# Hybrid decoder layer with a 32-expert feed-forward: Silu and one VectorE product per expert, and slot lists kept by place, the most-used expert at place 1, with 128 slots at every place

## The reference, cut to what matters

```python
logits = xf @ router_w + router_b                 # 512 tokens, 32 experts
top_val, top_idx = lax.top_k(logits, 4)
gates = softmax(top_val)
# for each expert e, over the tokens that chose it:
gu = xb @ mlp1_w[e] + mlp1_b[e]                   # 1024 -> 2048, gate and up interleaved
gate, up = minimum(gu[..., ::2], 7.0), clip(gu[..., 1::2], -7.0, 7.0)
act = (up + 1.0) * gate * sigmoid(1.702 * gate)
y = act @ mlp2_w[e] + mlp2_b[e]                   # 1024 -> 1024
out[token] += gates[token, e] * y
# then x + out, and a last rmsnorm
```

## Time and profile before

| | |
|---|---|
| timed runs, median of 3 | 1603.47 us (1601.67 to 1604.37) |
| span of the profiled execution, first to last instruction | 1602.2 us |
| PE busy | 1547.4 us, 97% |
| DVE busy | 1320.1 us, 82% |
| ACT busy | 1068.4 us, 67% |
| POOL busy | 347.6 us, 22% |
| DMA | 465.30 MB, mean 290 GB/s |
| weight pieces, issue to landing | 384, 1024 KB each, median 8.0 us |

### The profile page before, as it was taken

One profiled execution on the slowest core, in us unless ns is written; L12 is line 12 of the kernel. 1 busy time (PEld: TensorE's weight loads), 2 busy tenths in 40 slices (PEclk: granted clock), 3 DMA queues, 4 the chain that ended last, 5 costly groups with the idle time before them and its releaser, 6 DMA issues.

```text
span 1602.2 us, 27288 instructions
## 1 busy us (share of the span) xinstructions
PE 1547.4 (97%) x10197; PEld 1254.4 (78%) x10198; DVE 1320.1 (82%) x1101; ACT 1068.4 (67%) x1014; POOL 347.6 (22%) x278
## 2 busy tenths in 40 slices
PE   6899999987899999999999999999999999999997
PEld 5677777765778888888888888888888888888885
DVE  5556565656498999999999999999999999999996
ACT  4635353434367777777777777777777777777774
POOL 7100000001145322212222212222222222221210
PEclk9999999998999999999999999999999999999999
DMA  6211111006399999999999999999999999999993
GB/s 198 57 54 41 54 41 54 15 2 224 153 390 367 375 391 383 385 381 361 385 379 377 386 383 377 375 372 378 371 383 376 381 380 372 372 374 373 384 375 134
DMA packets 99101, 465.30 MB, mean 290 GB/s; under 512 B 11408, under 2 KB 38192, under 8 KB 49760
## 3 DMA queue, kind: packets, MB, share of 16 engines
q1 hardware_dynamic: 86176, 429.59, 68.7%
q0 software_dynamic: 12864, 34.85, 8.3%
HBM read 448.51 MB, written 22.69 MB: 294 GB/s over the span
## 4 chain that ended last, share of the span: by engine, by line
PE 73%; DVE 2%; DMA 1%; ACT 0%; issue 0%; DVEq 0%; POOLq 0%
PE psum L1932 29%; PE psum L1960 14%; PE psum L1935 14%; PE psum L1965 7%; PE psum L1330 3%; PE psum L1922 2%; PE psum L1914 2%; DVE w_pieces_lo L1754 1%; PE psum L1948 1%; DMA xg<-h_rows,gath_i 0%; DMA w_pieces<-in_mlp_w 0%; PE psum L1346 0%; PE psum L1338 0%; DVE x L1876 0%; DMA w_pieces<-in_w_out 0%
## 5 line engine op out<-in xcount | busy, mean ns | idle before, releaser
L1754 DVE TENSOR_TENSOR w_pieces_lo<-w_pieces,w_pieces_hi 128x2048 fp32r<-128x2048 f32 x384 | 867.6, 2288 | 79.8 <-ACT w_pieces_hi L1618 79.7
L1618 ACT ACTIVATE w_pieces_hi<-w_pieces 128x2048 fp32r<-128x2048 f32 x384 | 736.1, 1919 | 220.5 <-PE psum L1935 154.1
L1932 PE MATMUL psum<-w_pieces_hi,xh 128*128 128x512 f32 x1024 | 284.3, 399 | 0.0
L1932 PE MATMUL psum<-w_pieces_hi,xl 128*128 128x512 f32 x1024 | 274.4, 390 | 0.0
L1935 PE MATMUL psum<-w_pieces_lo,xh 128*128 128x512 f32 x1024 | 274.2, 389 | 0.0
L1558 POOL DMA_INDIRECT sum_rows<-ys,this_i x30 | 143.6, 4786 | 418.2 <-ACT ys L1638 417.9
L1932 PEld LDWEIGHTS psum<-w_pieces_hi,xl 128*128 128x128 f32 x1024 | 192.2, 188 | 41.3
L1935 PEld LDWEIGHTS psum<-w_pieces_lo,xh 128*128 128x128 f32 x1024 | 192.2, 188 | 40.3
L1932 PEld LDWEIGHTS psum<-w_pieces_hi,xh 128*128 128x128 f32 x1024 | 185.3, 188 | 45.1 <-issue 11.3
L1960 PE MATMUL psum<-w_pieces_hi,ah 128*128 128x512 f32 x512 | 158.0, 390 | 0.1
L1960 PE MATMUL psum<-w_pieces_hi,al 128*128 128x512 f32 x512 | 157.7, 389 | 0.0
(11 more groups left out here) (366 smaller groups left out, 1901.9 us busy)
## 6 DMA issues: line engine op xcount, KB each, us to landing
w_pieces<-in_mlp_w SPq DMA_DIRECT2D x384, 1024.0 KB, 8.0
w_raw<-in_w_in SPq DMA_DIRECT2D x26, 512.0 KB, 4.1
w_pieces<-in_w_out SPq DMA_DIRECT2D x8, 512.0 KB, 9.2
sum_rows<-x POOLq DMA_DIRECT2D x5, 512.0 KB, 3.7
chunk_work<-in_x SPq DMA_DIRECT2D x4, 512.0 KB, 6.1
sc<-pall POOLq DMA_DIRECT2D x16, 128.0 KB, 4.0
x<-in_x SPq DMA_DIRECT2D x4, 512.0 KB, 13.6
h_rows<-w_pieces POOLq DMA_DIRECT2D x4, 512.0 KB, 2.9
```

The costliest lines, as they stand in the source:

```text
L1618: nc.scalar.activation(hi[:, p % RING], raw[:, raw_slot(b, p)].rearrange("p r n -> p (r n)"), ACT.Copy).then_inc(s_hi, 1)
L1754: nc.vector.tensor_tensor(lo[:, p % RING], raw[:, raw_slot(b, p)].rearrange("p r n -> p (r n)"), hi[:, p % RING].bitcast(F32), ALU.subtrac ...
L1932: nc.tensor.matmul(bank(up_bank(b) + c), a[:, k, :], hi[:, p % RING, c * 512:(c + 1) * 512], start=False, stop=False)
```

## The change

- The activation: ACT takes `Silu` of 1.702*gate, which is 1.702*gate*sigmoid(1.702*gate), as soon as up is clipped. DVE takes min(silu, its value at 7) times the clipped up. The product with the clipped gate (L1778) is gone, and the factor 1.702 is taken out of the gates in routing.
- Places: the experts get places. Places 0, 30 and 31 keep their experts; of experts 1 to 29 the one with most tokens changes place with expert 1. `place_of_expert` and its twin `expert_at` hold the exchange (it is its own inverse). The list keys use the place, the weight loads of SP read the expert number of a place from `expert_at` into a register, and the one-hot column that picks an expert's bias comes from `pick_at` instead of a constant table.
- Widths: places 0 and 1 have `P` = 128 slots, all others `NARROW` = 128 slots. The code that is narrower for places from 2 on is there, with a width of 128. `lists` is loaded by two DMAs (places 0 and 1; 2 to 31). PE's turns b = 2 and 3 are written out, its loop runs from 4.

The core of the diff:

```diff
+WIDE = 2
+NARROW = 128
+SILU_MAX = float(ALPHA * 7.0 / (1.0 + np.exp(-ALPHA * 7.0)))
@@ output_and_route, route_vector
-        nc.vector.tensor_tensor(rank[:, :, 0:EXPERTS], hidden[:], ranks, ALU.add)
-        nc.vector.tensor_tensor(rank[:, :, INDEXED - 1:INDEXED], hidden[:, :, EXPERTS - 2:EXPERTS - 1], ranks[:, :, EXPERTS - 2:EXPERTS - 1], ALU.add)
-        chain(nc.vector.memset(r1[:, 29:30], 0.0))
+        nc.vector.tensor_tensor(rank_at[:, :, 0:1], hidden[:, :, 0:1], ranks[:, :, 0:1], ALU.add)
+        chain(nc.vector.tensor_tensor(rank[:], hidden[:], ranks, ALU.add))
         g["select"](0, 0)
...
-        chain(nc.vector.tensor_reduce(r1[:, 20:21], bank(5, NT * EXPERTS, (NT + 1) * EXPERTS), AX.X, ALU.max))
+        chain(nc.vector.scalar_tensor_tensor(largest[:], counts, float(EXPERTS), con("among"), ALU.mult, ALU.add))
+        chain(nc.vector.tensor_reduce(r1[:, 21:22], largest[:], AX.X, ALU.max))
+        chain(nc.vector.tensor_scalar(only[:], largest[:], r1[:, 21:22], None, ALU.is_equal))
+        chain(nc.vector.tensor_tensor_reduce(moved[:], only[:], con("experts"), 1.0, 0.0, ALU.mult, ALU.add, r1[:, 22:23]))
+        chain(nc.vector.tensor_tensor(moved[:], only[:], con("to_one"), ALU.mult))
+        chain(nc.vector.tensor_tensor(place_of_expert[:], moved[:], con("experts"), ALU.add))
+        chain(nc.vector.tensor_copy(place_of_expert[:, 1:2], r1[:, 22:23]))
+        nc.vector.tensor_scalar(gates[:], gates[:], 1.0 / ALPHA, None, ALU.mult)
+        for place in range(1, 3):
+            last = nc.vector.scalar_tensor_tensor(at_place[:, place - 1], over_tokens(place_of_expert[:]), float(place), rank[:], ALU.is_equal, ALU.mult)
+        chain(last)
+        nc.vector.tensor_copy(expert_at[:], place_of_expert[:]).then_inc(g["s_order"], 1)
+        nc.vector.tensor_scalar(pick_at[:, 0:EXPERTS], place_of_expert[:], con("lane"), None, ALU.is_equal).then_inc(g["s_order"], 1)
+        nc.vector.tensor_reduce(rank_at[:, :, 1:3].rearrange("p t n -> p n t"), at_place[:], AX.X, ALU.add)
+        nc.vector.tensor_copy(rank_at[:, :, LAST_COL:RANK_COLS], rank[:, :, EXPERTS - 2:EXPERTS])
+        chain(nc.vector.scalar_tensor_tensor(largest[:], only[:], float(NARROW - P), counts, ALU.mult, ALU.add))
+        chain(nc.vector.tensor_tensor(largest[:], largest[:], con("wide_first"), ALU.subtract))
+        chain(nc.vector.tensor_reduce(r1[:, 20:21], largest[:], AX.X, ALU.max))
@@ experts, sync
+            def expert(b):
+                return sp.value_load(expert_at[0:1, bass.ds(b, 1)], min_val=0, max_val=EXPERTS - 1)
...
+            sp.wait_ge(g["s_order"], 1)
+            e = expert(1)
...
             with sp.Fori(2, EXPERTS) as b:
-                for p in range(PIECES):
-                    load(r, b, p)
+                e = expert(b - 2)
+                for p in range(DOWN):
+                    load(r, b, p, e)
+                e = expert(b)
+                for p in range(DOWN, PIECES):
+                    load(r, b, p, e)
@@ experts, gpsimd
-            nc.gpsimd.dma_start(lists[:, 0:EXPERTS, :], g["list_dram"].rearrange("(r s e) w -> r s e w", s=P, e=EXPERTS)[bass.ds(r, 1)].rearrange(
-                "a s e w -> (a s) e w")).then_inc(s_lists, 16)
-            pool.wait_ge(s_lists, r * 16 + 16)
+            rows = g["list_dram"].rearrange("(s e) w -> s e w", e=EXPERTS)
+            nc.gpsimd.dma_start(lists[:, 0:WIDE, :], rows[bass.ds(r * P, P), 0:WIDE, :]).then_inc(s_lists, 16)
+            nc.gpsimd.dma_start(lists[0:NARROW, WIDE:EXPERTS, :], rows[bass.ds(r * NARROW, NARROW), WIDE:EXPERTS, :]).then_inc(s_lists, 16)
+            pool.wait_ge(s_lists, r * 32 + 32)
@@ experts, scalar and vector
-            nc.scalar.activation(sg[:], pairs(e)[:, :, 0], ACT.Sigmoid, scale=1.702).then_inc(s_sig, 1)
+            nc.scalar.activation(sg[:], pairs(e)[:, :, 0], ACT.Silu, scale=ALPHA).then_inc(s_sig, 1)
-            nc.vector.tensor_scalar(uu[:], pairs(e)[:, :, 1], 8.0, -6.0, ALU.min, ALU.max).then_inc(s_u, 1)
-            dve.wait_ge(s_u, r * EXPERTS + (e + 1))
-            nc.vector.scalar_tensor_tensor(uu[:], pairs(e)[:, :, 0], 7.0, uu[:], ALU.min, ALU.mult).then_inc(s_x, 1)
+            nc.vector.tensor_scalar(uu[:], pairs(e)[:, :, 1], 8.0, -6.0, ALU.min, ALU.max).then_inc(s_x, 1)
-            nc.vector.scalar_tensor_tensor(av[:], sg[:], SIG_MAX, uu[:], ALU.min, ALU.mult).then_inc(s_act, 1)
+            nc.vector.scalar_tensor_tensor(av[:], sg[:], SILU_MAX, uu[:], ALU.min, ALU.mult).then_inc(s_act, 1)
@@ experts, tensor
+        def width(b):
+            return P if isinstance(b, int) and b < WIDE else NARROW
-            with pe.Fori(2, EXPERTS) as b:
+            for b in range(2, 2 + WIDE):
+                down(r, b)
+                up(r, b, True)
+            with pe.Fori(2 + WIDE, EXPERTS) as b:
```

More of the change, by code:

```diff
@@ L1114, in output_and_route @@
     stacked = carve(P, NT, 4 * EXPERTS).rearrange("p t (c e) -> p t c e", c=4).bitcast(F32R)
+    largest = carve(P, EXPERTS)
+    only = carve(P, EXPERTS)
+    moved = carve(P, EXPERTS)
+    place_of_expert = carve(P, EXPERTS)
+    at_place = carve(P, 2, NT, EXPERTS)
     w_v = d["w_out"][0].rearrange("(k p) n -> p k n", p=P)
@@ L1414, in experts @@
 def experts(nc, d, sb, sem, st, g, route, con, ident, psum, bank, out):
-    rank, info, flags, raw, bias, s_raw = (g[k] for k in ("rank", "info", "flags", "raw", "bias", "s_raw"))
+    rank_at, expert_at, pick_at, info, flags, raw, bias, s_raw = (g[k] for k in ("rank_at", "expert_at", "pick_at", "info", "flags", "raw", "bias", "s_raw"))
     x, stat, o_t, sum_dram, down_b, turned = (g[k] for k in ("x", "stat", "o_t", "sum_dram", "down_b", "turned"))
@@ L1640, in pick_bias @@
         def pick_bias(r, m):
-            nc.scalar.activation(pick[:], con("pick")[:, bass.ds(m, 1)].to_broadcast([P, P]), ACT.Copy).then_inc(s_pick, 1)
+            if not isinstance(m, int) or m:
+                act.wait_ge(g["s_order"], 2)
+            column = con("pick") if isinstance(m, int) and not m else pick_at[:, bass.ds(m, 1)]
+            nc.scalar.activation(pick[:], column.to_broadcast([P, P]), ACT.Copy).then_inc(s_pick, 1)
         def first_split():
-            nc.scalar.activation(stat[:, 54:55], con("eps"), ACT.Sigmoid)
+            nc.scalar.activation(stat[:, 54:55], con("eps"), ACT.Silu)
             pick_bias(0, 0)
@@ L1904, in _, with first @@
         pe.sem_inc(s_ta, 1)
+        def first(b):
+            return isinstance(b, int) and b < 2
         def index_sum(r, m):
@@ L1939, in up_bias @@
             pe.wait_ge(s_pick, r * TURNS + (b + 1))
-            if isinstance(b, int) and b == 1:
+            if first(b) and b == 1:
                 pe.wait_ge(s_xh, (r * TURNS + 1) * 2 + 1)
@@ L1947, in up_bias @@
                 for half, rows in enumerate((slice(0, 64), slice(64, 128))):
-                    nc.tensor.matmul(bank(up_bank(b) + 2 * half + c), pick[rows, :], bias[rows, c * 512:(c + 1) * 512], start=True, stop=False)
-            if isinstance(b, int):
+                    nc.tensor.matmul(rows_of(up_bank(b) + 2 * half + c, width(b)), pick[rows, 0:width(b)], bias[rows, c * 512:(c + 1) * 512], start=True, stop=False)
+            if first(b):
                 pe.wait_ge(s_xh, (r * TURNS + b) * 2 + 1)
@@ L1954, in down_piece @@
         def down_piece(r, b, p, into=0):
+            m = width(b - 2)
             n = r * STREAM + (place(b, p) + 1)
@@ L1985, in up @@
             for p in range(DOWN, PIECES):
-                if p == 8 and first:
+                if p == 8 and early:
                     pe.wait_ge(s_xh, (r * TURNS + b) * 2 + 2)
                 up_piece(r, b, p)
-                if p == 6 and first and act:
+                if p == 6 and early and act:
                     pe.wait_ge(s_x, r * EXPERTS + 2)
@@ L1992, in up @@
                     turn_x(r, b, 1, 3)
-                if p == (7 if first else 5) and act:
+                if p == (7 if early else 5) and act:
                     turn_a(r, b - 1, 0, 2)
-                    turn_a(r, b - 1, 1, 1 if first else 3)
+                    turn_a(r, b - 1, 1, 1 if early else 3)
                 if p == 6 and not act:
```

96 lines of the change are left out of this document (56 added, 40 removed).

## The result

The changed kernel takes 1607.44 us in the median of 10 runs (1604.67 to 1610.73), the kernel before 1603.62 us in 10 runs beside it (1601.67 to 1604.63). The ratio is 1.0025 with a 95% interval of 1.0016 to 1.0034: 3.8 us slower, where 1.4 us were forecast. The profiled execution has a span of 1606.5 us, 4.3 us more than before.

A forecast was written before the change was run, and what follows sets the result against it. PE was taken to bound the loop, with DVE beside it up to 470 us. Loop, Silu, register loads and lists counted 0, routing +1.4 us: 1603.5 + 1.4 = 1604.9 us, range 1602.0 to 1608.5.

The forecast's parts named there:

- rival 2: DVE is the true bound of the loop; 38 us would go, to 1566 us; chance 0.04.
- The estimate of 5.3 us more on ACT: Loop: by the skill's table-set rule, Silu and copies in two sets cost ACT 5.3 us per expert, within 8.4 us rest.
- The length of the addition: Routing ahead of `sel` of expert 1: 17 more instructions take 3.6 us, bounds 2.6 to 5.
- DVE's path: From `sel` to `xl` of expert 1: waits absorb 2.2 of 3.6 us, so expert 1's bias comes 1.4 us later.
- PE's own path: PE's index sum and transposes behind `sel` of expert 1: PE starts expert 0 0.9 us later, smaller than DVE's path.
- term (a): PE's index sum waits for the later `sel` of expert 1, so PE starts expert 0 0.9 us later.
- term (b): DVE's work from `sel` to `xl` of expert 1 runs 1.4 us late, and expert 1's bias with it.
- I take 0.9 us more, hidden: List loads: the second DMA adds issue and landing time, 0.9 us, covered before PE needs the low part.
- The slack of 1.9 us: Behind the lists: the low part is done at 519.5 us, PE needs it at 521.33, so 1.9 us are free.
- costed at 0: Loop: removing one 1.22 us DVE instruction per expert lies beside PE's work and changes the time by 0.
- Rival 3: The lists' two small DMAs land late and delay PE; 1607.8 us with doubled landing, 2.9 us more; chance 0.15.
- Rival 4: A per-turn cost breaks through, SP register load or ACT table switch; 0.2 us per turn gives 1611 us; chance 0.06.

The follow-up runs named there:

- e1: The kernel before with Silu and without the second DVE product, the gates scaled by one more short DVE instruction; 1603.52 us, ratio 1.0001.
- e9: The kernel before with 18 one-element DVE steps added behind `sel` of expert 1; 1604.81 us, ratio 1.0018.
- e3: The changed kernel with the lists loaded by one DMA instead of two; 1607.09 us, ratio 1.0019 to the kernel before.
- e5: The kernel before with 18 one-element DVE steps added ahead of `sel`, right before the largest-count reduction; 1605.29 us, ratio 1.0014.
- e7: The changed kernel with ACT's copy of the previous expert's output moved from piece 7 to piece 10; 1608.70 us, ratio 1.0026 to the kernel before.
- e8: The kernel before with Silu and without the second product, plus the output copy moved to the turn's end; 1604.98 us, ratio 1.0014.
- e11: The changed kernel with PE's turns 2 and 3 back inside its loop; 1606.96 us, ratio 1.0024 to the kernel before.

## Why the prediction was right and wrong

**The loop and Silu: right.** A turn of 35.42 us (35.43 in the mean, see below), Silu at 1026 ns, no table load in the loop, DVE's work down by 34.0 us, and e1 at 1.0001. DVE was not the hidden bound (rival 2). At the end DVE's wait in front of the last `al` grew from 2.01 us to 3.25, as the forecast had it, and SP still waits 857.7 us in all for free slots (894.2 before), so its register loads are covered there:

```profile
1572.77 0.69 DVE L1821 TENSOR_TENSOR al<-psum,ah 128x512 fp32r<-128x512 f32 x1 [3.25 <-ACT ah L1680]
```

```profile
SPq L1525 <- DVE w_pieces_lo L1805: 857.7, 378, 10.5
```

The estimate of 5.3 us more on ACT put Silu and the copies into two table sets. The sections of the Trainium skill that it names don't put them so, and the trace has no such switch in the loop.

**The length of the addition: right.** 3.34 us for 3.6; chained short steps take 0.19 us and 0.03 more, and L1324's read of the sum 0.08.

**What of it reaches PE: DVE's path about right, PE's own path too cheap.** 1.4 us were forecast by DVE's path, with PE's index sum as the smaller one at 0.9. Measured are 1.19 us, and 1.12 to 1.58 in the six kernels with the new routing. DVE's path gives 1.11 us of it: `xl` of expert 1 starts 35.68 us behind the count before and 36.79 in the changed kernel.

```profile
470.10 0.68 DVE L1764 TENSOR_TENSOR xl<-psum,xh 128x512 fp32r<-128x512 f32 x1
```

```profile
472.17 0.69 DVE L1815 TENSOR_TENSOR xl<-psum,xh 128x512 fp32r<-128x512 f32 x1
```

e9 gives that path alone 0.90. PE's path has 0.52 us of lateness (transposes 10.71 us behind the count, 10.19 before) and 0.83 us by the clock, less the 0.20 us that PE waited at bias 1 before: 1.15 us. In the changed kernel both arrive together (bias 1 has no recorded wait and starts 0.22 us behind the end of `xl`). The term that was missing is the clock. It made term (a) as large as term (b), and in e3, e5 and e7, where bias 1 starts 0.48 to 0.64 us behind the end of `xl`, larger.

**The lists: the step that failed.** "I take 0.9 us more, hidden" was to cover all the lateness of the lists. Measured are 3.54 us more (`this_f` at 10.12 us behind bias 2 for 6.58), of which 1.86 us reached PE. The slack of 1.9 us was read about rightly, but in one profile whose lists were early: the other profile of before has used it up already. And one source of lateness was counted, the second DMA, where there are three:

- The removed product, 0.94 us on POOL, which I had costed at 0 because PE and ACT don't wait for it; POOL was never asked.
- The wait for the placing DMAs' landing, 5.16 us for 5.08, and 4.80 to 6.64 in all profiles.
- The second DMA with the landing of the lists, 7.34 us for 4.83. It is 6.47 to 7.34 us in the six profiles with two DMAs (mean 6.92), 3.76 to 6.85 in the eight with one (mean 5.75), so that a good part of these 2.51 us can be chance.

The last column of the ledger orders the stalls: with `this_f` 5.4 to 6.6 us behind bias 2 the two turns lose nothing, at 8.2 and 8.3 they lose 0.6 to 0.8, at 8.9 1.3, at 9.7 to 10.2 1.4 to 2.4, at 11.0 2.8 us (e7 and e8 apart, where the gather decides). Rival 3 named this mechanism and priced it at 2.9 us for a doubled landing. The measured 1607.4 us lies near its 1607.8 and not near the forecast's 1604.9; the range held it only because it reached up to that rival.

**Per turn.** Rival 4 is there in a size that I had not thought of: 13 ns in every turn from bias 4 on, 0.36 us in all. It goes with the change of places (all six kernels that have it, no other), not with PE's written-out turns (e11). Whether SP's register loads or something else makes it was not tried and stays open.

**The sum.** 1.19 + 1.86 + 0.36 = 3.4 us, the 0.96 us ahead of the count and the -0.07 make the 4.3 us between the two spans; the medians differ by 3.8. The ledger explains two executions, not the medians: e1 has 1.44 us of stall in its profile and none in its median. Against the other profile of before, which has a stall of 0.79 of its own, the lists' part would be 1.1 us. How the stall divides in the median among the three sources stays open. No kernel here beats the one before.

## What to carry to other kernels

Ask of a removed instruction not only who waited for it but who worked beside it: a short DVE read of PSUM between long SBUF splits was the window in which POOL could issue. A slack that hangs on small DMAs under load is to be read from more than one profile, because a landing of 4.8 us was 6 to 7 us in most others. An experiment on such a slack needs more than one profile too. And a late start can cost more than its lateness where the granted clock has fallen: here 0.52 us of lateness came with 0.83 us at the lower level.
